# Working the first turn of the input projection on the unnormed input, and scaling its four banks behind it

## The reference, cut to what matters

```
def rmsnorm(x, g):
    y = x * rsqrt(mean(x * x, axis=-1) + EPS)
    return y * g

h = rmsnorm(x, norm1_g)
z = h @ w_in + b_in                       # 1024 -> 2*1024 + 1280 + 1280 + 1024 + 1024
z_glu, z_rx, z_rg, z_ga, z_gb = split(z)
u = z_glu[..., :1024] * sigmoid(z_glu[..., 1024:])
u = causal_depthwise_conv(u, conv_dw_w, conv_dw_b)      # 31 taps
```

## Time and profile before

| | |
|---|---|
| median of three runs | 2342.3 us (2341.27 to 2345.14) |
| profiled execution, on the device | 2340.96 us |
| its span | 2339.1 us |
| TensorE busy | 2298.2 us, 98% |
| VectorE busy | 1031.5 us, 44% |
| ScalarE busy | 898.0 us, 38% |
| GpSimd busy | 1037.6 us, 44% |
| mean granted clock of TensorE | 0.986 of full |

### The profile page before, as it was taken

How to read it: one execution, slowest core, us unless ns; L and a number is a source line. 1 busy time by engine, 2 the same in 40 slices (tenths; PEclk the granted TensorE clock), 3 DMA queues, 4 the chain that set the end, 5 groups by cost and what they waited for, 6 DMA issues and landing times.

```text
span 2339.1 us, 33586 instructions
## 1 busy us (share of the span) xinstructions
PE 2298.2 (98%) x10800; PEld 1897.0 (81%) x10800; DVE 1031.5 (44%) x1669; ACT 898.0 (38%) x1621; POOL 1037.6 (44%) x784
## 2 busy tenths in 40 slices
PE   8999999999999999999999999999999999999997
PEld 7888888888888888888888678888677788888886
DVE  6899886446514314100126235555765565110112
ACT  4334663333222233332332354445555552332331
POOL 3455553454444443444454443333223462444443
PEclk8999999999999999999999999999999998999998
DMA  4333444338737432333332223334212431333331
GB/s 151 95 94 105 143 119 142 98 120 298 268 99 241 159 90 73 94 99 99 94 95 68 82 79 110 111 111 161 69 50 60 152 95 49 95 99 98 93 101 54
DMA packets 129483, 263.96 MB, mean 113 GB/s; under 512 B 14256, under 2 KB 14384, under 8 KB 128624
## 3 DMA queue, kind: packets, MB, share of 16 engines
q1 hardware_dynamic: 119520, 236.51, 33.3%
q10 hardware_dynamic: 9872, 26.25, 3.0%
HBM read 250.02 MB, written 12.58 MB: 112 GB/s over the span
## 4 chain that ended last, share of the span: by engine, by line
PE 75%; issue 13%; POOL 6%; DVE 5%; ACT 1%; DMA 0%; POOLq 0%; ACTq 0%; DVEq 0%
PE bank L977 23%; PE bank L978 23%; PE bank L979 23%; POOL wlo L411 6%; PE bank L1328 1%; PE bank L1394 1%; PE bank L1372 1%; PE bank L1119 1%; DVE bank L1647 1%; PE bank L1143 1%; PE bank L1052 0%; PE bank L1127 0%; PE bank L1070 0%; PE bank L1103 0%; DMA cols<-d_cols 0%
## 5 line engine op out<-in xcount | busy, mean ns | idle before, releaser
L411 POOL TENSOR_TENSOR wlo<-raw,whi 128x512 fp32r<-128x512 f32 x750 | 1000.8, 1340 | 1239.6 <-ACT whi L474 1238.8
L977 PE MATMUL bank<-a_hi,whi 128*128 128x512 f32 x1928 | 764.2, 396 | 9.2 <-DVE a_lo L1453 6.8
L979 PE MATMUL bank<-a_lo,whi 128*128 128x512 f32 x1928 | 752.7, 390 | 0.0
L978 PE MATMUL bank<-a_hi,wlo 128*128 128x512 f32 x1928 | 752.5, 390 | 0.0
L474 ACT ACTIVATE whi<-raw 128x512 fp32r<-128x512 f32 x750 | 469.0, 627 | 685.5 <-PE bank L979 609.7
L977 PEld LDWEIGHTS bank<-a_hi,whi 128*128 128x128 f32 x1928 | 363.1, 188 | 92.1 <-DVE a_lo L1453 10.5
L979 PEld LDWEIGHTS bank<-a_lo,whi 128*128 128x128 f32 x1928 | 363.2, 188 | 76.7
L978 PEld LDWEIGHTS bank<-a_hi,wlo 128*128 128x128 f32 x1928 | 363.3, 188 | 75.8 <-issue 1.4
L977 PE MATMUL bank<-b_hi,whi 128*128 128x512 f32 x852 | 335.0, 393 | 0.6 <-DVE b_lo L1785 0.3
L978 PE MATMUL bank<-b_hi,wlo 128*128 128x512 f32 x852 | 331.6, 389 | 0.0
L979 PE MATMUL bank<-b_lo,whi 128*128 128x512 f32 x852 | 331.5, 389 | 0.0
(11 more groups left out here) (264 smaller groups left out, 1886.1 us busy)
## 6 DMA issues: line engine op xcount, KB each, us to landing
raw<-d_stream SPq DMA_DIRECT2D x750, 256.0 KB, 2.6
G<-d_ada SPq DMA_DIRECT2D x72, 512.0 KB, 4.5
spill_rv<-tmp ACTq DMA_DIRECT2D x32, 256.0 KB, 2.1
G<-spill_rv ACTq DMA_DIRECT2D x8, 1024.0 KB, 8.3
G<-d_x ACTq DMA_DIRECT2D x4, 512.0 KB, 5.6
spill_ga<-sq ACTq DMA_DIRECT2D x8, 256.0 KB, 3.7
G<-spill_ga ACTq DMA_DIRECT2D x1, 2048.0 KB, 8.3
G<-d_x ACTq DMA_DIRECT2D x1, 2048.0 KB, 13.6
```

The lines of the kernel that those rows point to most:

```text
L411: pool.tensor_tensor(wlo[:, s % SRING, :], raw[:, s % RING, :], whi[:, s % SRING, :].bitcast(F32), ALU.subtract).then_inc(lo_done, 1)
L977: pe.matmul(out_ps, w_hi, hi[:, k, :], start=first and q == 0, stop=False)
L978: pe.matmul(out_ps, w_lo, hi[:, k, :], start=False, stop=False)
L979: mm = pe.matmul(out_ps, w_hi, lo[:, k, :], start=False, stop=last and q == len(ks) - 1)
```

## The change

The parameters are loaded ahead of x, the masks behind ScalarE's squares. ScalarE first makes b_hi, the high half of x * gain, without the root; VectorE makes b_lo beside it (the buffers of operand B, which are free then). TensorE does panels 0 to 3 of the first turn with these, then the sums (one group of four one-column matmuls, since VectorE now adds all eight squares), panel 4, the broadcast, and panels 5 to 7. The fillers behind the sums and the ordering by input tile are gone. VectorE then makes operand A as before, for the turns that follow, and in the same loop copies the broadcast to a5, multiplies each of the four banks by it in place (`scale_first`), and makes the first two gated products (`gated`), which stood behind the constants before. ScalarE does the first two sigmoids inside its loop of a_hi, and the constants' Abs, Exp and Silu behind that. The counts of b_hi_w and opb move by the 8 new tiles. Everything else is unchanged, the loads of the stream by SyncE too.

```diff
--- before.py
+++ after.py
...
@@ -554,24 +555,41 @@
                 ffn_gates(f"gu{n}b", FB // 2)
                 ffn_down(f"dn{n}b", FB, norm, False)
+            act.dma_start(cols[:, :], cols_d).then_inc(ld_cols, 16)
             for j in range(4):
                 act.dma_start(X[:, 2 * j:2 * j + 2, :], xT[:, 2 * j:2 * j + 2, :]).then_inc(ld_x[j], 16)
             act.dma_start(consts[:, :, :], consts_d).then_inc(ld_c, 16)
-            act.dma_start(cols[:, :], cols_d).then_inc(ld_c, 16)
-            act.dma_start(G[:, 0:8 * P], masks_d.rearrange("p a b -> p (a b)")).then_inc(ld_m, 16)
             act.wait_ge(const_ready, 1)
+            act.wait_ge(ld_cols, 16)
             for k in range(KD):
                 if k % 2 == 0:
                     act.wait_ge(ld_x[k // 2], 16)
+                act.activation(b_hi[:, k, :], X[:, k, :], ACT.Copy, scale=col("norm1_g", k)).then_inc(b_hi_w, 1)
+                if k in (0, 2):
+                    split("win", 0, k // 2)
+            for k in range(KD):
                 first_square(k, X[:, k, :])
-            act.wait_ge(ld_c, 32)
+                if k in (2, 5):
+                    split("win", 0, 2 + k // 5)
+            act.dma_start(G[:, 0:8 * P], masks_d.rearrange("p a b -> p (a b)")).then_inc(ld_m, 16)
+            tick("win", 0, 1, 4)
+            def first_sigmoid(pr):
+                act.wait_ge(raw_scaled, 2 * pr + 2)
+                act.activation(R5[:, pr, :], bank[2 * pr + 1][:, :], ACT.Sigmoid, bias=col("b_in", 2 * pr + 1))\
+                   .then_inc(evac[2 * pr + 1], 1)
+            for k in range(KD):
+                if k in (2, 6):
+                    first_sigmoid(k // 4)
+                act.wait_ge(a_val, k + 1)
+                act.activation(a_hi[:, k, :], tmp[:, k % 2, :], ACT.Copy).then_inc(a_hi_w, 1)
+                if k in (1, 3, 5):
+                    tick("win", 0, 5 + k // 2, 1)
             own.next(act.activation(lru_t[:, 0, :], cols[:, COLS["lru_lambda"][0]:COLS["lru_lambda"][0] + KR], ACT.Abs))
             act.activation(lru_t[:, 1, :], lru_t[:, 0, :], ACT.Exp, scale=-1.0).then_inc(lam_e, 1)
             act.activation(small[:, 7, 0:8], cols[:, COLS["c_2"][0]:COLS["c_2"][0] + 8], ACT.Silu).then_inc(silc, 1)
-            for s in range(AHEAD):
-                split("win", 0, s)
-            round_a("h1", 0, name="win")
             def begin_taps(m):
@@ -585,11 +603,11 @@
                    .then_inc(first_taps, 1)
                 act.activation(odd, U[:, m + 1, 1:1 + T], ACT.Copy, scale=col("conv_dw_w", 8 + m)).then_inc(first_taps, 1)
-            for i in range(4):
+            for i in range(1, 4):
                 for pr in range(2):
                     for j in range(2 * pr, 2 * pr + 2):
-                        wide_tick("win", i, j, 0 if i else 4)
-                    if i and not pr:
+                        wide_tick("win", i, j)
+                    if not pr:
                         begin_taps(i)
                     wait_used(act, "win", i, 5 + 2 * pr)
@@ -1095,15 +1113,6 @@
                 broadcast(n + 1, src=ROOT2, dst=bank[6])
                 keep_warm(22)
-            def sum_pairs():
-                for j in range(4):
-                    pe.wait_ge(pair_ready, j + 1)
-                    for tt in range(4):
-                        mm = pe.matmul(AUX[:, tt:tt + 1], SQ_FIRST[:, 2 * j, tt * P:(tt + 1) * P], ones[:, 0:1],
-                                       start=(j == 0 and tt == 0), stop=(j == 3 and tt == 3), skip_group_check=True)
-                    mm.then_inc(sq_summed, 2)
             def sum_both(k):
                 pe.wait_ge(sq_ready, 8 * NORM["nf"] + k + 1)
@@ -1171,10 +1180,20 @@
             pe.wait_ge(const_ready, 1)
             keep_warm(14)
-            sum_pairs()
-            broadcast(1, warm=8)
-            keep_warm(10)
-            wide_stage("win", OPA, opa, FILL_A["h1"], 9)
+            raw = (opb, FILL_B["raw"])
+            for j in range(4):
+                bank_free("win", 0, j)
+                panel("win", 0, j, range(4), bank_of("win", j)[:, :], OPB, True, False, ready=raw if j == 0 else None)
+            pe.wait_ge(pair_ready, KD - 1)
+            for tt in range(4):
+                mm = pe.matmul(AUX[:, tt:tt + 1], SQ_FIRST[:, 0, tt * P:(tt + 1) * P], ones[:, 0:1], start=tt == 0,
+                               stop=tt == 3, skip_group_check=True)
+            mm.then_inc(sq_summed, 8)
+            for j in range(4):
+                panel("win", 0, 4 + j, range(4, 8), bank_of("win", j)[:, :], OPB, False, True, ready=raw if j == 0 else None)
+                if j == 0:
+                    broadcast(1)
+            wide_stage("win", OPA, opa, FILL_A["h1"], 9, later=1)
             def lru_gates(half):
@@ -1593,21 +1612,61 @@
                 dve.memset(small[:, 4, 0:1], 0.0).then_inc(s, 1)
                 dve.wait_ge(s, 1)
             dve.memset(small[:, 5, 0:1], 0.0).then_inc(const_ready, 1)
-            dve.wait_ge(ld_c, 32)
-            for s in ld_x:
-                dve.wait_ge(s, 16)
-            for j in range(4):
-                dve.wait_ge(sq_ready, 2 * j + 2)
-                dve.tensor_tensor(SQ_FIRST[:, 2 * j, :], SQ_FIRST[:, 2 * j, :], SQ_FIRST[:, 2 * j + 1, :], ALU.add).then_inc(pair_ready, 1)
+            dve.wait_ge(ld_cols, 16)
+            for k in range(KD):
+                dve.wait_ge(b_hi_w, FILL_B["raw"] + k + 1)
+                dve.scalar_tensor_tensor(out=b_lo[:, k, :], in0=X[:, k, :], scalar=col("norm1_g", k),
+                                         in1=b_hi[:, k, :].bitcast(F32), op0=ALU.mult, op1=ALU.subtract).then_inc(opb, 1)
             own.next(dve.memset(one_g2[:, :, 0:1], 1.0))
             g = cols[:, COLS["norm_f_g"][0]:COLS["norm_f_g"][0] + KD]
             own.next(dve.tensor_tensor(one_g2[:, :, 1], g, g, ALU.mult))
-            dve.wait_ge(ld_m, 16)
-            own.next(dve.tensor_copy(masks[:, :, :].rearrange("p a b -> p (a b)"), G[:, 0:8 * P]))
-            own.next(dve.memset(U[:, :, 0:PAD], 0.0))
+            def take_masks():
+                dve.wait_ge(ld_m, 16)
+                own.next(dve.tensor_copy(masks[:, :, :].rearrange("p a b -> p (a b)"), G[:, 0:8 * P]))
+                own.next(dve.memset(U[:, :, 0:PAD], 0.0))
             own.next(dve.memset(XR[:, :, 0:LPAD], 0.0))
-            norm_stat(NORM["n1"])
-            operand_a("h1", lambda k: col("norm1_g", k))
+            for k in range(1, KD):
+                dve.wait_ge(sq_ready, k + 1)
+                dve.tensor_tensor(SQ_FIRST[:, 0, :], SQ_FIRST[:, 0, :], SQ_FIRST[:, k, :], ALU.add).then_inc(pair_ready, 1)
+                dve.wait_ge(pair_ready, k)
+            dve.wait_ge(ld_c, 16)
+            dve.wait_ge(sq_summed, 8)
+            rsqrt(AUX[:, 0:4], 4, 1.0 / D, st_ready)
+            stat[0] += 1
+            take_masks()
+            dve.wait_ge(bc_ready, stat[0])
+            def scale_first(j):
+                wait_used(dve, "win", 0, 4 + j)
+                dve.tensor_tensor(bank[j][:, :], bank[j][:, :], a5[:, :], ALU.mult).then_inc(raw_scaled, 1)
+            def gated(m):
+                i, j = m // 2, m % 2
+                dve.wait_ge(evac[2 * j + 1], i + 2)
+                dve.scalar_tensor_tensor(out=U[:, m + 1, PAD:U_ST], in0=bank[2 * j][:, :], scalar=col("b_in", 2 * m),
+                                         in1=R5[:, j, :], op0=ALU.add, op1=ALU.mult).then_inc(evac[2 * j], 1)
+                dve.wait_ge(evac[2 * j], i + 2)
+            for k in range(KD + 1):
+                if k < KD:
+                    if k > 1:
+                        dve.wait_ge(opa, FILL_A["h1"] + k - 1)
+                    dve.scalar_tensor_tensor(out=tmp[:, k % 2, :], in0=X[:, k, :], scalar=col("norm1_g", k), in1=BCAST[:, :],
+                                             op0=ALU.mult, op1=ALU.mult).then_inc(a_val, 1)
+                if k:
+                    lo_a("h1", k - 1)
+                if k == 1:
+                    own.next(dve.tensor_copy(a5[:, :], BCAST[:, :]))
+                if k in (1, 5):
+                    scale_first(k // 2)
+                    scale_first(k // 2 + 1)
+                if k in (3, 7):
+                    gated(k // 4)
+            filled["a"] = FILL_A["h1"] + KD
             dve.wait_ge(lam_e, 1)
             w, w2, acc = (lru_t[:, r, :] for r in (0, 2, 3))
@@ -1661,11 +1720,9 @@
             taps = 0
             for m in range(KD):
-                i, j = m // 2, m % 2
-                dve.wait_ge(evac[2 * j + 1], i + 2)
-                dve.scalar_tensor_tensor(out=U[:, m + 1, PAD:U_ST], in0=bank[2 * j][:, :], scalar=col("b_in", 2 * m),
-                                         in1=R5[:, j, :], op0=ALU.add, op1=ALU.mult).then_inc(evac[2 * j], 1)
-                dve.wait_ge(evac[2 * j], i + 2)
+                j = m % 2
+                if m > 1:
+                    gated(m)
                 more = 5 * TAPS if m == KD - 1 else taps + (20 if j else 6)
                 conv_run(taps, more)
```

(7 more changed lines are left out.)

## The result

The changed kernel took 2356.4 us, the median of four runs (2355.96 to 2360.32), against 2343.1 for the kernel before beside it: a ratio of 1.0064, interval [1.0051, 1.0076]. The forecast was 2349.9 with a range to 2355.0.

A forecast was written before the change was run, and what follows sets the result against it. TensorE bounds the opening, but VectorE decides its third turn: operand A at 33.4 plus 44.5 us puts that turn 8.3 us late; 2341.0 + 8.3 = 2349.3, with half of 1.3 on top 2349.9 us; range 2344.0 to 2355.0.

The forecast's parts named there:

- The mechanism: VectorE starts operand A 10.2 us later, so its third gated product delays TensorE's third turn by 8.3 us; chance 0.77.
- 44.5 + 0.7 + 0.3: VectorE from operand A to the third gated product's start, 44.5 us; then that product, then TensorE's start.
- The forecast's marks: Timeline signs: stream load at 10.1, first matmul at 15.3, operand A at 33.4, no matmul between about 67 and 78.9.
- rival (a): Third turn doesn't wait for VectorE, TensorE's bound holds: 3.2 us faster, 2338.4 us; chance 0.07.
- rival (c): Clock stays at 1.2 GHz until VectorE starts operand A, 12 us later than the sum: 2361.9 us; chance 0.05.
- The first failed step: Norm: seven VectorE additions of squares at 0.69 us each, over by 25.3, hidden by panels 1 to 3.
- The step that the forecast did add for GpSimd at the root: Norm's root on VectorE: one tiny step slowed by a GpSimd low half, 1.25 us instead of 0.17.
- The second failed step: TensorE's granted clock: up at 20.8, 5.5 us after the first panel starts, panels 1 to 3 done by 28.9.
- 8.3: Delay of TensorE's third turn in us: start at 78.9 instead of 70.57, with all that follows shifted whole.
- 12.4 us of low clock at the first panel: Upper bound for the clock's rise after the first panel starts, against 5.5 taken: 3.5 us more.
- half of the port's cost on operand A: GpSimd's low halves delaying VectorE's operand A subtractions: 1.4 us taken, 3.9 at most; the range took half of 2.5.

The follow-up runs named there:

- e3: Changed kernel without the seven VectorE additions of squares (a tiny memset for each, norm over one tile of eight): 2353.7 us, ratio 1.0055.
- e8: Changed kernel with ScalarE's splits of panels 4 to 7 held back until the seventh addition is over: 2356.6 us, ratio 1.0057.
- a0: The changed kernel itself, measured and traced a second time: 2359.4 us, ratio 1.0069 to the kernel before.
- e4: Changed kernel with 20 filler matmuls on TensorE between panel 3 and the sums: 2358.2 us, ratio 1.0076.
- e5: Changed kernel with ScalarE's splits moved out of its loop of copies, one behind every second square: 2352.1 us, ratio 1.0044.
- b2: Kernel before, with VectorE's constants computed a second time ahead of the third gated product: 2350.3 us, ratio 1.0037.
- b1: Kernel before, with VectorE's constants moved behind the last gated product: 2339.4 us, ratio 0.9988.
- e1: Changed kernel with VectorE's constants moved behind the last gated product: 2344.5 us, ratio 1.0017.
- e10: Changed kernel, squares first, constants late, earlier norm, 20 taps ahead of the third gated product, scalings and first products inside operand A's loop: 2338.6 us, ratio 0.9980.
- e2: Changed kernel with 13 of the 26 taps ahead of the third gated product moved later: 2350.8 us, ratio 1.0045.
- e6: Changed kernel, squares first, constants late, earlier norm, 20 taps ahead of the third gated product, scalings and products behind operand A's loop: 2346.2 us, ratio 1.0018.
- e9: Changed kernel with squares ahead of the first splits and constants behind the last gated product: 2338.2 us, ratio 0.9983.

## Why the forecast was right in its direction and too small

**The mechanism held.** Third turn minus start of operand A was forecast as 44.5 + 0.7 + 0.3 = 45.5 us. It was 45.7 in the changed kernel, e3, e8 and a0, and 44.6 in e4 and e5. The path is right, and that the number fits so closely is luck: two terms missed by about 2.2 us each, in opposite directions. From operand A's start to its end, with the two products, it was 15.9 us where the forecast's terms leave 18.2 (one subtraction was slow and not two, the scalings took less, no sigmoid was waited for). The constants took 11.3 us where it kept 9.1, since low halves met six of their steps instead of four. The forecast's marks came in this way: stream issued at 10.5 (10.1), first panel at 15.21 (15.3), no matmul from 73.8 to 85.96 (67 to 78.9), a wait of 1.8 us at bank 2 (3.7). The loads were costed nearly rightly (the stream 1.1 us later for 0.7), the masks were there in time, the constants and taps stood where the forecast had them, and nothing was given back later: rival (a), TensorE's bound, never decided. The low clock of rival (c) was not one unbroken stretch, as written there; it came back behind the two long waits, of 4.3 and 12.2 us, and not behind those of 1.8 and 1.3.

**The first failed step is the additions': "The seven additions on VectorE (0.69 each, by a_lo's 24.67 row) follow the squares and are over by 25.3, hidden by panels 1 to 3."** They took 1.64 us in the median and were over at 32.14. The forecast's own rows had the price, 1.37 where 0.69 is usual and 1.25 where 0.17 is the earlier trace rows, and it counted a delay by GpSimd for the root and for operand A. It didn't ask which low halves stand beside the additions. They are those of panels 3 to 7: ScalarE splits them between 22.13 and 28.66 with waits of 0.5 and 2.1 us only, and GpSimd works them off from 22.82 to 30.87 with 0.3 us of idle time, without any for the last four (row below; alone they take 1.30 each).

```profile
24.39 6.48 POOL L412 TENSOR_TENSOR wlo<-raw,whi 128x512 fp32r<-128x512 f32 x4 [0.27 <-ACT whi L475]
```

In such a stretch the additions take turns with the low halves. That cost TensorE 4.3 us. The step that the forecast did add for GpSimd at the root (1.1 us) didn't come: GpSimd was idle by then, and the root's steps took 0.16 to 0.17 us each.

**The second failed step is the clock.** The forecast asked how late it would rise at the first panel, and not what an idle TensorE would do to it later. At the first panel it was better than forecast: 1.00 from 18.5 instead of 20.8, so that panel 3 ended at 27.95 instead of 28.9. In a0 it rose only at 21.1, and the wait for the additions was 3.4 us instead of 4.3: since they decide, an earlier clock there gains nothing. But from 32.2, after the wait, it was 0.50 until 39.0. From the resumption at 32.20 to operand A at 40.27 it took 8.1 us where 4.5 had been forecast. e4's trace gets 2.3 of these 3.6 back by fillers alone. So operand A's 6.9 us are -1.0 (earlier clock) + 4.3 (additions) + 3.6 (mostly clock). The forecast also let TensorE stand idle for 11.5 us ahead of the third turn and let it resume at full clock: it resumed at half, from 85.96 to 90.2, which is 4.2 / 2 = 2.1 us. b2 shows the same behind a wait of only 4.5 us.

**The sum then.** 8.3 + 7.1 (third turn at 85.96 instead of 78.9) + 2.1 (clock behind the wait) = 17.5 us, against 19.4 between the two profiled executions (that of the changed kernel, 2360.3, is the slowest of its four runs) and 13.3 and 18.1 between the medians. What is left against 19.4 is mostly one stretch, shown below. That the distances of two measurements of one kernel stand 5 us apart (13.3 and 18.1) is not explained by the opening, whose rows repeat; that it is the clock of the runs, as within one measurement, is likely and not shown.

**The range** was built from single bounds: 12.4 us of low clock at the first panel and half of the port's cost on operand A. Neither is what happened. A bound for the additions at the slow rows' price, 7 x 0.7 us more, would have been in the rows, and so would a drop of the clock behind an idle stretch of 11 us.

## What to carry to other kernels

Work that fills a start-up gap of one engine is paid on another: list what the engine that prepares operands must do before it frees the first bank that is reused, and move from there what nobody needs yet. Here the early first turn lost 13 to 18 us until the constants and the squares had been moved; then it was 3.4 us faster than the kernel before, of which the moved constants alone give 2.2 (b1). When an elementwise step is called hidden, look up which GpSimd instructions run beside it, and when a forecast contains a long idle stretch of TensorE, let it resume at half clock: it did so behind each of the 13 waits of 3.4 to 12.2 us that these traces have between the first panel and 100 us.

## What the runs showed of the hardware

An addition of two SBUF tiles on VectorE took 0.69 us alone and 1.64 to 1.68 in alternation with GpSimd's subtractions, and these became slower too, 1.43 to 1.74 us instead of 1.30. The Trainium skill (SBUF — State Buffer, Who interferes with whom) says that VectorE's instructions with two SBUF inputs contend with GpSimd's reads, and that the later one waits for the whole of the other. The additions agree roughly: 0.69 plus 0.95 of a low half's 1.30. The low halves lengthened by only 0.13 to 0.44, less than an addition's 0.69, so an addition and a low half together took 1.70 us (the additions start at 24.70, 26.40, 28.10), where one behind the other would take 1.99. The root's steps of e8 agree too: the three that were slow have two SBUF inputs of 128x4 elements and took 1.20 to 1.21 us instead of 0.16, so the delay has the size of GpSimd's instruction and not of VectorE's own.

The granted clock can be 0.50 behind a short wait, and in one execution but not in the next. In the profiled execution of the changed kernel, at a norm some 290 us behind the opening, TensorE waited 0.9 us, and the window that begins 1.5 us behind this wait has 0.50 (timeline, then window):

```profile
375.48 1.05 PE L1070 MATMUL bank<-ones,G 128*128 128x1 f32 x8 [0.89 <-DVE G L1711]
```

```profile
377.00:380.20 3.20, 3.20 (x9) 2.52 (x8) 0.43 (x1) 0.00 (x0) 0.00 (x0) 0.50 0.97 396
```

The kernel before has the same wait (0.9 us, at 358.0) and passes what follows at 1.00. The stretch lasts from 376.9 to 380.3 and costs half of that, 1.7 us. The wait is in all 14 traces; the low clock behind it is in eight (the changed kernel twice, e1, e3, e8, b1, b2, e10) and not in six (before, e2, e4, e5, e6, e9). Behind the wait of 1.8 us for the second gated product it was 0.50 for 3.4 us in e4 and e5 and stayed at 1.00 in the changed kernel. What decides it the rows don't show. There are more such stretches later: behind 100 us the traces have between 45.7 us (e1, e4, e10) and 60.1 us (b2) at half clock, the kernel before 52.8, the changed kernel 56.5. Half of 14.4 us is 7.2: by this estimate two profiled executions can differ by up to 7 us that are not the edit's.
